# Streams' stage of a streaming encoder: joint queries, two-part moving operands, fp32 rotary keys, and one tile of the next stage moved into its end

## The reference

```python
q = einsum('btr,rhe->bthe', rms_norm(cq, q_g), w_uq)          # 8 heads, 64 + 32 wide
q_lat = einsum('bthn,lhn->bthl', q[..., :64], w_uk)           # into the latent space, 128 wide
q_rope = rope(q[..., 64:], pos)
s = (einsum('bqhl,bkl->bhqk', q_lat, ckv) + einsum('bqhr,bkr->bhqk', q_rope, kr)) * MLA_SCALE
o_lat = einsum('bhqk,bkl->bqhl', softmax(s), ckv)             # keys: 16 meta, 1024 cached, 16 new
o_swa = softmax over 16 meta + 128 cached + 16 new keys and a sink, times the SWA values
o_a = einsum('bthl,lhv->bthv', o_lat, w_uv)
mix = concatenate([rms_norm(o_a, g_a), rms_norm(o_swa, g_b)])
x = layer_norm(ALPHA * x + mix @ w_out)
```

## Time and profile before

| | |
|---|---|
| median of 3 runs | 3587.97 us (3578.82 to 3598.31) |
| profiled execution, own time | 3592.09 us |
| its span in the profile | 3590.1 us |
| mean granted TensorE clock | 0.918 of 2.4 GHz |
| busy: PE / DVE / ACT / POOL | 3189.0 / 1628.6 / 851.5 / 857.2 us |
| stage E, layer 0 | about 608 to 763 us of the span |
| stage E, layer 1 | about 2378 to 2527 us |

### The profile page before, as it was taken

The page is one execution under the profiler, slowest core; times in us unless marked ns, Lnnn a source line. Parts: engine busy times, 40 slices in busy tenths (PEclk is TensorE's granted clock), DMA queues, the critical chain, the costliest instruction groups (busy, mean ns, idle before and its releaser), DMA issues. The chain is left out here.

```text
span 3590.1 us, 46713 instructions
## 1 busy us (share of the span) xinstructions
PE 3189.0 (89%) x18498; PEld 2903.1 (81%) x18498; DVE 1628.6 (45%) x2914; ACT 851.5 (24%) x1600; POOL 857.2 (24%) x695
## 2 busy tenths in 40 slices
PE   1978888989899999999849688889889999999995
PEld 0966666877799999999849566668769999999995
DVE  6446777646322222222355577756463222222226
ACT  1323333522311111111123233335222111111111
POOL 1222333631111121111012233337111121111111
PEclk9987998679999999999969898967889999999997
DMA  5221112421211011110033211034111111111101
GB/s 194 86 92 40 30 30 60 148 84 60 77 41 35 35 47 47 41 41 23 38 114 107 73 38 31 24 102 146 63 66 54 35 53 41 41 41 35 35 23 65
DMA packets 117587, 219.02 MB, mean 61 GB/s; under 512 B 33088, under 2 KB 70720, under 8 KB 116752
## 3 DMA queue, kind: packets, MB, share of 16 engines
q1 hardware_dynamic: 106656, 185.51, 15.8%
q0 software_dynamic: 10800, 31.73, 2.3%
HBM read 177.08 MB, written 42.46 MB: 61 GB/s over the span
## 5 line engine op out<-in xcount | busy, mean ns | idle before, releaser
L2087 PE MATMUL PS<-xh,fwh 128*128 128x390 f32 (+1 forms) x2112 | 718.5, 340 | 6.7 <-DVE fwl L2031 6.7
L2088 PE MATMUL PS<-xl,fwh 128*128 128x390 f32 (+1 forms) x2112 | 722.3, 342 | 0.0
L2089 PE MATMUL PS<-xh,fwl 128*128 128x390 f32 (+1 forms) x2112 | 721.6, 342 | 0.0
L2055 DVE TENSOR_TENSOR acc<-acc,PS 128x390 f32<-128x390 f32 x528 | 295.7, 560 | 495.6 <-PE PS L2089 495.6
L2042 DVE TENSOR_TENSOR gate<-PS,gate 128x390 f32<-128x390 f32 x132 | 74.4, 564 | 748.3 <-PE PS L2089 748.3
L2087 PEld LDWEIGHTS PS<-xh,fwh 128*128 128x128 f32 x2112 | 398.8, 189 | 7.5 <-issue 6.9
L2088 PEld LDWEIGHTS PS<-xl,fwh 128*128 128x128 f32 x2112 | 398.7, 189 | 0.6
L2089 PEld LDWEIGHTS PS<-xh,fwl 128*128 128x128 f32 x2112 | 397.9, 188 | 0.0
L2087 PE MATMUL PS<-hidh,fwh 128*128 128x390 f32 (+1 forms) x1056 | 358.4, 339 | 4.5 <-DVE hidl L2046 4.5
L2089 PE MATMUL PS<-hidh,fwl 128*128 128x390 f32 (+1 forms) x1056 | 359.4, 340 | 0.0
L2088 PE MATMUL PS<-hidl,fwh 128*128 128x390 f32 (+1 forms) x1056 | 358.8, 340 | 0.0
(11 more groups left out here) (434 smaller groups left out, 5790.7 us busy)
## 6 DMA issues: line engine op xcount, KB each, us to landing
raw<-in_W_FF SPq DMA_DIRECT2D x88, 512.0 KB, 3.2
fraw<-in_W_FF SPq DMA_DIRECT2D x44, 512.0 KB, 3.2
raw<-in_W_IN SPq DMA_DIRECT2D x16, 592.0 KB, 4.9
ht<-out_H SPq DMA_DIRECT2D x18, 512.0 KB, 4.9
sqt_scratch<-sqTs POOLq DMA_DIRECT2D x18, 512.0 KB, 3.9
mt<-mix_scratch SPq DMA_DIRECT2D x18, 512.0 KB, 4.3
hc<-out_H SPq DMA_DIRECT2D x18, 512.0 KB, 3.7
out_H<-yo POOLq DMA_DIRECT2D x18, 512.0 KB, 3.0
```

Of the source, the lines that this page charges most:

```text
L2055: dve.tensor_tensor(a, a, Tb[e % 2][:, 0:NT[i]], ALU.add).then_inc(S("f_y"), 1)
L2087: pe.matmul(out, wh, mh, start=start, stop=False)
L2088: pe.matmul(out, wh, ml, start=False, stop=False)
L2089: return pe.matmul(out, wl, mh, start=False, stop=stop)
```

## The change

In stage E, and where it touches A and C:

- Queries: both token sets in one moving operand of 144 columns (`cq` holds high and low parts side by side, so that wuqh runs against 288 columns); `q_rope`, `q_nope`, `q_latent` with the two heads of a pair on the halves of the rows (`both_heads`). The rest of a product lands in other columns and is added by one more DVE operation (`qrest`).
- Rotary part: queries and keys stay fp32 on 32 rows (`qrT`, `dkr`, `krT`), without split and without copies; the split `krs` of stage A is gone, and so are ACT's and DVE's work on `drs`.
- Values: nine blocks of `dv` as stationary operand, high part against [P_hi, P_lo] (256 columns), low part against P_hi; the sums of the two column halves are joined by DVE (`orest`). The blocks of 32 keys lie in the same buffer, its other rows filled by a broadcast load. One split on ACT and one on GpSimd for all eleven blocks.
- W_OUT slices: two are split ahead of the loop, four in turns 3, 6, 8 and 9 on GpSimd, two on DVE in turns 8 and 9.
- C's tile 0: `mix_sq`, `mix_root`, `mix_norm`, `mix_T`, `mix_hi`, `mix_lo` in turns 7 to 9, `w_out(0)` between `project(0)` and `project(1)`, whose results go to the YB[1] bank; tile 1's norm is made ahead of the barrier.
- DVE's `keys_hi(1)` stands behind `bias(0)`; the loads of parameters and of two W_OUT slices stand ahead of the values' loads.

The diff, cut to its core:

```diff
+QT = P + META
+W_OUT_LATER = {3: 2, 6: 3, 8: 4, 9: 6}
+W_OUT_DVE = (5, 7)
+W_OUT_GROUP = (0, 0, 1, 1, 2, 2, 2, 2)
...
                     if b >= 2:
                         sp.wait_ge(S("s_done"), U(l, b - 2) + 1)
                     sp.dma_start(dkraw[i][:, :], CKVT[l, b]).then_inc(sem, 16)
-                    for j in range(3):
-                        sp.dma_start(drraw[i][ROPE * j:ROPE * (j + 1), :], KRT[l, b]).then_inc(sem, 16)
+                    sp.dma_start(dkr[i][:, :], KRT[l, b]).then_inc(sem, 16)
                     for j in range(2):
...
-                    sp.dma_start(dtraw[i][0:META, 0, :], CKV[l, b, PAST:CKEYS, :]).then_inc(sem, 16)
-                    sp.dma_start(dtraw[i][META:META + NS, 0, :], KVS[l, r0:r0 + NS, 0:LAT]).then_inc(sem, 16)
-                    sp.dma_start(dtraw[i][0:META, 1, :], SV[l, b, P:WKEYS, :]).then_inc(sem, 16)
-                    sp.dma_start(dtraw[i][META:META + NS, 1, :],
+
+                    sp.dma_start(dvraw[i][META + NS:P, 9:11, :],
+                                 CKV[l, b, 0:P - META - NS, :].rearrange("p (a n) -> p a n", a=1)
+                                 .to_broadcast([P - META - NS, 2, LAT])).then_inc(sem, 16)
+                    sp.dma_start(dvraw[i][0:META, 9, :], CKV[l, b, PAST:CKEYS, :]).then_inc(sem, 16)
+                    sp.dma_start(dvraw[i][META:META + NS, 9, :], KVS[l, r0:r0 + NS, 0:LAT]).then_inc(sem, 16)
+                    sp.dma_start(dvraw[i][0:META, 10, :], SV[l, b, P:WKEYS, :]).then_inc(sem, 16)
+                    sp.dma_start(dvraw[i][META:META + NS, 10, :],
                                  KVS[l, r0:r0 + NS, LAT + ROPE + KVH * HD:KVW]).then_inc(sem, 16)
...
+                load_params(sp, l, "E")
                 stream_keys(0)
                 for i in range(2):
                     sp.dma_start(f(sqT[i][:, :]), SQT[8 + i, :, 0:SWA_H * rows(8 + i)]).then_inc(S("sq_in"), 16)
-                load_params(sp, l, "E")
+                w_out_load(0)
+                stream_keys(1)
+                w_out_load(1)
                 stream_values(0)
-                stream_keys(1)
                 stream_values(1)
-                w_out_load(0)
-                w_out_load(1)
...
+                sp.wait_ge(S("c_mixn"), A(l, 0) + 1)
+                sp.dma_start(mt[:, :], MIX[cols(1), :]).then_inc(S("mt_in"), 16)
                 barrier(sp, phase_no(l, "E"))
 
                 for t in range(1, TILES + 1):
-                    if t < TILES:
+                    if 2 <= t < TILES:
                         sp.wait_ge(S("c_mixn"), A(l, t))
...
-                    pool.tensor_tensor(dvl[i][:, :, :], dvraw[i][:, :, :], f(dvh[i][:, :, :]), ALU.subtract)
-                    pool.wait_ge(S("dt_hi"), l * NB + b + 1)
-                    pool.tensor_tensor(dtl[i][:, :, :], dtraw[i][:, :, :], f(dth[i][:, :, :]), ALU.subtract)\
+                    pool.tensor_tensor(dv[i][:, 1, :, :], dvraw[i][:, :, :], f(dv[i][:, 0, :, :]), ALU.subtract)\
                         .then_inc(S("ds_rest"), 1)
...
                 keys_lo(0)
                 keys_lo(1)
+                w_out_lo(0)
+                w_out_lo(1)
                 for n in range(UNITS + 2):
                     if 1 <= n <= NB:
                         values_lo(n - 1)
                     if n + 2 < NB:
                         keys_lo(n + 2)
+                    if n in W_OUT_LATER:
+                        w_out_lo(W_OUT_LATER[n])
+                    if n in (8, 10):
+                        mix_root(n // 2 - 4)
                     if n >= 2:
                         store_window(n - 2)
-                    if n < KD:
-                        w_out_lo(n)
-                def mix_root(t):
...
-                    act.wait_ge(S(f"dm_in{i}"), 16 * 6 * (l * NB // 2 + b // 2 + 1))
-                    act.activation(dkh[i][:, :], dkraw[i][:, :], ACT.Copy)
-                    act.activation(drs[i][0:96, :], drraw[i][:, :], ACT.Copy).then_inc(S("dm_hi"), 1)
+                    act.wait_ge(S(f"dm_in{i}"), 16 * 4 * (l * NB // 2 + b // 2 + 1))
+                    act.activation(dkh[i][:, :], dkraw[i][:, :], ACT.Copy).then_inc(S("dm_hi"), 1)
 
                 def values_hi(b):
                     i = b % 2
-                    act.wait_ge(S(f"ds_in{i}"), 16 * 6 * (l * NB // 2 + b // 2 + 1))
-                    act.activation(dvh[i][:, :, :], dvraw[i][:, :, :], ACT.Copy).then_inc(S("ds_hi"), 1)
...
                 q_nope_hi(0)
+                q_nope_hi(1)
                 keys_hi(0)
-                q_rope_hi(0)
-                q_nope_hi(1)
                 q_latent_hi(0)
                 q_turned(0)
-                q_rope_hi(1)
+                q_latent_hi(1)
                 keys_hi(1)
                 params(act, (l, "E"))
                 soft(0)
-                q_latent_hi(1)
+                w_out_hi(0)
                 q_turned(1)
+                w_out_hi(1)
                 for n in range(UNITS + 2):
                     if 1 <= n <= NB:
                         values_hi(n - 1)
...
-                        w_out_hi(n)
-                mix_sq(0)
+                    for k in {2: (2,), 5: (3,), 7: (4, 5), 8: (6, 7)}.get(n, ()):
+                        w_out_hi(k)
+                    if n == 7:
+                        mix_sq(0)
+                    if n == 9:
+                        mix_hi(0)
+                        mix_sq(1)
...
+                def keys_hi(b):
                     i = b % 2
-                    dve.wait_ge(S(f"dm_in{i}"), 16 * 6 * (l * NB // 2 + b // 2 + 1))
-                    dve.tensor_copy(dsh[i][:, :, 0, :], dsraw[i][:, :, :])
-                    dve.wait_ge(S("dm_hi"), l * NB + b + 1)
...
+                def q_nope_lo(half):
+                    a, b = q_nope_halves(half)
+                    m = slice(2 * half, 2 * half + 2)
+                    dve.wait_ge(S("qa_hi"), QN(l, half) + 1)
+                    dve.scalar_tensor_tensor(out=qrest[:, m, :], in0=a, scalar=MLA_SCALE, in1=f(qnh[:, m, :]),
+                                             op0=ALU.mult, op1=ALU.subtract).then_inc(S("qa_rest"), 1)
+                    dve.wait_ge(S("qa_rest"), QN(l, half) + 1)
+                    dve.scalar_tensor_tensor(out=qnl[:, m, :], in0=b, scalar=MLA_SCALE, in1=qrest[:, m, :],
...
+                    if U(l, n):
+                        dve.wait_ge(S("out_read"), U(l, n))
+                    rest = orest[:, :].rearrange("p (h t) -> p h t", t=NS)
+                    dve.tensor_tensor(rest, o_view(n, 0), f(out_view(olh, ol9[0], n)), ALU.subtract).then_inc(S("o_rest"), 1)
+                    dve.wait_ge(S("o_rest"), U(l, n) + 1)
+                    dve.tensor_tensor(out_view(oll, ol9[1], n), o_view(n, 1), rest, ALU.add).then_inc(S("out_read"), 1)
...
-                keys_lo(0)
+                q_nope_lo(1)
                 q_rotate(1)
-                q_nope_lo(1)
+                params(dve, (l, "E"))
+                dve.tensor_scalar(nsink[:, :], sinkT[:, 4:5], -1.0, None, ALU.mult).then_inc(S("nsink"), 1)
+                keys_hi(0)
                 q_latent_lo(0)
-                q_rope_lo(1)
-                keys_lo(1)
+                q_latent_lo(1)
                 bias(0)
+                keys_hi(1)
                 inverse(0)
-                q_latent_lo(1)
                 for n in range(UNITS + 2):
-                    if 1 <= n <= NB:
-                        values_hi(n - 1)
...
+                    if n == 8:
+                        mix_norm(0)
+                        w_out_lo(5)
+                    if n == 9:
+                        mix_lo(0)
+                        w_out_lo(7)
+                mix_norm(1)
...
+                def q_nope(half):
+                    for m in (2 * half, 2 * half + 1):
+                        w = slice(m * P, m * P + P)
+                        out = q_nope_at(m)
+                        both = cq[:, :, :, :].rearrange("p k a n -> p k (a n)")
+                        pe.matmul(out, wuqh[:, 0, w], both[:, 0, :], start=True, stop=False)
                         for kk in range(2):
-                            ins = three(out[:, m * P:m * P + r], wuqh[:, kk, m * P:m * P + P], wuql[:, kk, m * P:m * P + P],
-                                        cq[i][:, 0, kk, :], cq[i][:, 1, kk, :], kk == 0, kk == 1)
+                            pe.matmul(out[:, 0:QT], wuql[:, kk, w], cq[:, kk, 0, :], start=False, stop=False)
...
-                        keys(s[:, TAIL:TAIL + META], dkh[b][:, PAST:CKEYS], dkl[b][:, PAST:CKEYS], drs[b][0:96, PAST:CKEYS])
-                        keys(s[:, TAIL + META:TAIL + META + NS], ckvTh[:, o:o + NS], ckvTl[:, o:o + NS], krT[0:96, o2:o2 + NS])
+                        keys(s[:, TAIL:TAIL + META], dkh[b][:, PAST:CKEYS], dkl[b][:, PAST:CKEYS], dkr[b][:, PAST:CKEYS])
+                        keys(s[:, TAIL + META:TAIL + META + NS], ckvTh[:, o:o + NS], ckvTl[:, o:o + NS], krT[:, o2:o2 + NS])
                         for c in (slice(0, BANK), slice(BANK, 2 * BANK)):
```

(93 more changed lines are left out.)

271 lines of the change are left out of this document (122 added, 149 removed).

## The result

The changed kernel takes 3635.18 us (median of 4 runs, 3630.47 to 3639.47), the kernel before 3589.21 us beside it: a ratio of 1.0129, 95% interval 1.0097 to 1.0160. That is 46 us more, where 21 us less was forecast, and 23 us above the end of the range. The profiled execution took 3639.5 us (span 3637.6).

A forecast was written before the change was run, and what follows sets the result against it. Bound by TensorE's own instructions, over half the time at the slow clock; per stage 0 - 1.3 - 3.8 + 1.4 - 7.0 = -10.7 us, two stages -21.4, from 3588.0 to 3566 us; 8-in-10 range 3530 to 3612.

The forecast's parts named there:

- Rotary keys in fp32: Score sets: fp32 on 32 rows costs four fp32r passes, taken as upper bound; +3.0 us low, +1.6 high per `scores`.
- the clock term: Streams' stage: 70% instead of 63% of loop work at the high level, -3.5 us, and the end partly there, -3.5.
- (b): Rival, loop: clock stays low behind fp32 score runs, 25% of work at high level; +19 us a stage, 3619; chance 0.18.
- The start: Stage's start, up to stream 2's scores: earlier scores(0) against dearer scores and a `dsh` wait; 0, between -4 and +4 us.
- Values: Value sets: two wider matmuls per block instead of three, -1.92 us low, -1.01 high; price after 5.8 and 3.2 us.
- GpSimd's waits: Loop: TensorE's waits on GpSimd, 4.8 and 7.3 us in the two layers, taken as gone; -6.0 us.
- The end and stage C: Last two value sets -3.8 us; C's tile 0 moved ahead of the barrier +1.4, idle behind it staying.
- The clock term of -3.5: Stage's end: wider value sets let its 11.6 us run partly at the high level; -3.5 us.
- (c): Rival: fp32 on 32 rows costs no more than fp32r (-19 us a stage), or over 90% high (-12); 3529 to 3543; 0.15.

The follow-up runs named there:

- e3: Changed kernel with the scores' rotary matmul in fp32 over 128 rows, latent rows standing in for the rotary part: 3574.5 us, ratio 0.9951.
- e1: Changed kernel with the scores' rotary matmul as one fp32r pass over 32 rows, latent rows standing in: 3577.0 us, ratio 0.9954.
- e6: Changed kernel with the scores' rotary matmul in fp32 over 64 rows, latent rows standing in: 3627.4 us, ratio 1.0086.
- e11: Changed kernel with the scores' rotary matmul in fp32 over 96 rows, latent rows standing in: 3572.3 us, ratio 0.9959.
- e9: Changed kernel with all four matmuls of a score set as one fp32r pass over 32 rows, rotary part left out: 3556.6 us, ratio 0.9909.
- e10: Changed kernel with all four matmuls of a score set as one fp32r pass over 64 rows, rotary part left out: 3548.7 us, ratio 0.9893.
- e12: Changed kernel with 64 rows of zeros added to its fp32 rotary keys and queries, making 96 rows, nothing left out: 3576.4 us, ratio 0.9959.
- e2: Changed kernel with the scores' rotary matmul as one fp32r pass over 96 rows, latent rows standing in: 3542.5 us, ratio 0.9870.

## Why the prediction was wrong

**The step that failed** is the one headed "Rotary keys in fp32", with the clock term that was built on it. Its passes were right: four, 1.71 us against 0.43 in e3, +1.28 us as taken, and one load more on 16 columns; the Trainium skill, FP8 and Floating Point Precision, section TensorE Precision Notes, has the four passes too. What the sum did not have is a second price: the step from 128 rows to 32 and back, 0.59 us a long set and 0.19 a short one. The stack of before stood on 96 rows and paid none. Each stream pays 3.0 us for passes and 1.57 for steps at the low level, 4.6 where 3.0 was forecast. The forecast took four times one pass as the upper bound of the fp32 matmul, and it was none. The Trainium skill, TensorEngine Tiling (Array Packing), section Key Properties, says that a change of tiling mode drains TensorE. e1 and e6 agree with it, if fewer rows are such a change, and give the cost, 0.59 us; in e11 96 rows cost nothing extra.

No row of before shows the step in a score set, but its value sets do, whose blocks of 32 keys stand among blocks of 128. It is in the stretch that the prediction read as "33 of them in 7.70 us (686.55 to 694.25, some gaps among them)", timeline of before:

```profile
691.42 0.41 PE L2089 MATMUL PS<-PTh,dvl 128*128 128x128 f32 x1
691.77 0.47 PE L2087 MATMUL PS<-PTh,dth 32*128 32x128 f32 x1
692.04 0.41 PE L2088 MATMUL PS<-PTl,dth 32*128 32x128 f32 x1
692.25 0.41 PE L2089 MATMUL PS<-PTh,dtl 32*128 32x128 f32 x1
692.60 0.47 PE L2087 MATMUL PS<-dvh,PTh 128*128 128x128 f32 x1
692.87 0.41 PE L2088 MATMUL PS<-dvl,PTh 128*128 128x128 f32 x1
```

The pace is 0.213 us; at each change of rows the starts are 0.35 and 0.27 apart, 0.19 to 0.20 more, some 0.4 there and back. The gaps were the price that the sum lacked.

**The clock** was taken to rise from 63% to 70% of the loop's work at the high level. It fell to 0.61, under the 0.65 at which the prediction called itself wrong and (b) right. (b)'s direction and place were right: the high level no longer comes back in or behind the score runs. Its reason, a quarter of the rows at work, is borne out in part: with few rows in all four matmuls and no step inside a set it does not come back there either (e9, e10), and rows of zeros bring it back (e12). With few rows in one of four, as in the changed kernel, it is these rows or the gaps of the step; no run parts the two. (b)'s number came near by luck. The 22 us at the high level are 2.2 of six turns at the forecast's 10.0 us, 37% of the work, where (b) had 25% for its +19 us; at 37% its own rule gives +13. The other 3.8 turns, at 18.3 + 1.57 for the steps, make 76 us, 98 together by this estimate, and the loop took 100.4: the steps, which (b) did not have, made up most of what the clock did not.

By stages in layer 0: passes +19.7 (e3 on e2), few rows in one matmul +23.7 (e1 on e2, 12.6 the step's price and 11 clock), together 43.4 of the 46.2 that part the changed kernel from e2.

**The start** was forecast at 0, and is +0.5, by terms that were off in both directions: scores(0) came 11.1 us in, not 15, since the joint queries and latents ran at the high level from 607.8 us on (window 607.8 to 614.6, clock 1.00); the wait of 3.29 us on `dsh` is there; and scores(2) waits 4.38 us more. Ahead of it ScalarE's `keys_hi(2)` stands behind `q_turned(1)`, for which ScalarE idles 9.49 us, and behind `w_out_hi(1)`, GpSimd's work behind `w_out_lo(1)`; the forecast named the last two and gave them no price.

**Values.** Right: 18 matmuls on `dv`, and the set at the low level takes 5.7 us (762.36 to 768.08), 5.8 forecast, the high one 3.4 (696.31 to 699.70), 3.2 forecast. **GpSimd's waits** were forecast at nothing; 5.4 us (5.0 in layer 1) came back as one wait, by that order on ScalarE. **The end and stage C**: `w_out(0)` stands at 777.79, ahead of the barrier, and the idle behind the barrier stayed, as forecast. But the end is -0.4 instead of -5.9. The clock term of -3.5 came in part: stream 6's values took 4.39 us (752.18 to 756.57, clock 0.73) where the low level takes 5.7, and the stretch up to `w_out(0)` has 0.59 (749.21 to 777.79) where before it was 0.50 throughout (731.30 to 771.71). What took the gain are waits: that one of 5.41 us and one of 1.21 us on `mn` ahead of `mix_T(0)`, against one of 1.16 us on `dtl` that is gone.

Without the price of the fp32 keys the forecast is -10.7 - 19 = -29.7 us a stage, 59 in both (the 19 stand in (c)); e2, which pays none and has none of the stack's work on ScalarE and VectorE either, has -24.3 in layer 0 and 47 by the medians. The fp32 keys were to cost 38 of these 59 us and cost 93. So of the error of 67 us (from -21 to +46) some 55 are in the edit that the prediction called the one against the change, and 12 in all the rest.

## What to carry to other kernels

- In an accumulation group keep the number of rows on one side of the line between 64 and 96: a small contraction among full ones costs 0.59 us a round trip at 1.2 GHz with 512 columns, and, in this kernel, about as much again through the clock. Pad it with rows of zeros, or stack something useful into them, before counting its passes.
- A change that saves work on every other engine can cost time when TensorE is 89% busy: price its instructions first, both neighbours of a new one included.
- Gaps in a run of equal matmuls are a price: see what changes at them before calling them gaps. The steps of 0.2 us in the value sets of before foretold the one in the score sets.
- A wait by order (a cast behind two others that nobody waits for yet) is found in the row of the idle engine: GpSimd's 6.44 us idle on ScalarE's `dv`.

## What the runs showed of the hardware

- fp32 takes four passes of fp32r for 512 columns on 96 and 128 rows (1.71 against 0.43 us at 1.2 GHz), two loads instead of one for 16 columns (a set of four 1.07 against 0.85 us), and shows as two records. On 32 and 64 rows the set is longer by the step's 0.59 us, as with fp32r.
- A matmul of 512 columns on 32 rows between ones on 128 costs 0.56 + 0.72 + 0.59 us where 0.43 each is the pace, and the fp32 one on 64 rows the same 0.59 more in all; on 96 rows it costs nothing extra. With 128 columns a step costs 0.2 us each way (before).
- Behind score sets on 96 or 128 rows the transposes ran at a granted clock of 1.00 in e3 and 0.88 to 1.00 in e11 and e12; behind sets with 32 or 64 rows, in one matmul or in all four, at 0.50 to 0.61. Rows of zeros acted as rows of data did (stage clock 0.71 in e12, e11 and e3).
- How the clock's loss in the changed kernel splits between the few rows and the gaps stays open, as do the 9 us between the stages of its profile.
